# Sub-keys of two heads in the mask buffer, and four cache copies tied to expert rows, in a one-core decoder step

## What is computed

```
def peer_ffn(h, w_pq, sub_keys, expert_u, expert_v):
    t = h.shape[0]
    q = (h @ w_pq).reshape(t, PEER_HEADS, 2, PEER_D_KEY // 2)
    s = jnp.einsum('thcd,hcnd->thcn', q, sub_keys).astype(jnp.float32)
    s_top, i_top = lax.top_k(s, PEER_TOPK)
    ...
    expert = i1 * PEER_N_KEYS + i2
    g = jax.nn.softmax(c_top, axis=-1)
    u = expert_u[expert]
    act = jax.nn.gelu(jnp.einsum('thkd,td->thk', u, h))
    return jnp.einsum('thk,thkd->td', (g * act).astype(h.dtype), expert_v[expert])
```

## Time and profile before

| what | value |
|---|---|
| median of 3 runs | 1177.81 us (1176.51 to 1186.96) |
| the profiled execution's own time | 1179.88 us |
| its span | 1178.2 us |
| TensorE busy | 907.9 us (77%) |
| VectorE busy | 609.7 us (52%) |
| GpSimd busy | 409.9 us (35%) |
| moved by DMA | 481.44 MB, mean 409 GB/s |
| of it on queue q0 / q1 | 378.58 / 102.23 MB |

### The profile page before, as it was taken

How to read it: one execution, slowest core, us unless ns; L and a number is a source line. 1 busy time by engine, 2 the same in 40 slices (tenths; PEclk the granted TensorE clock), 3 DMA queues, 4 the chain that set the end, 5 groups by cost and what they waited for, 6 DMA issues and landing times.

```text
span 1178.2 us, 13121 instructions
## 1 busy us (share of the span) xinstructions
PE 907.9 (77%) x3725; PEld 425.4 (36%) x3725; DVE 609.7 (52%) x1604; ACT 333.3 (28%) x946; POOL 409.9 (35%) x432
## 2 busy tenths in 40 slices
PE   2799997678778758887877768677868777887785
PEld 0343334443334445543433434222323332333231
DVE  2200102543225625665555565566777777777766
ACT  1000004631220114323323232232333333333343
POOL 1202333122320202342434234433555445454542
PEclk9999999787988978998989898898998989989987
DMA  9999999999999998999999999999999999999997
GB/s 362 421 413 388 408 400 410 402 394 386 393 404 405 338 386 317 417 442 417 423 428 429 428 428 434 423 447 410 427 427 419 428 428 427 428 427 428 428 416 313
DMA packets 71747, 481.44 MB, mean 409 GB/s; under 512 B 9769, under 2 KB 10250, under 8 KB 26002
## 3 DMA queue, kind: packets, MB, share of 16 engines
q0 software_dynamic: 55008, 378.58, 77.8%
q1 hardware_dynamic: 16658, 102.23, 21.4%
q10 hardware_dynamic: 32, 0.02, 0.0%
HBM read 477.55 MB, written 70.32 MB: 465 GB/s over the span
## 4 chain that ended last, share of the span: by engine, by line
DMA 46%; PE 31%; issue 8%; DVE 7%; POOL 4%; ACT 3%; SPq 1%; POOLq 0%; DVEq 0%; ACTq 0%
DMA R<-in_uv,idst 33%; PE ps L1028 11%; PE ps L622 6%; DMA R<-in_sb_v,vrow 5%; POOL R L492 3%; DMA R<-in_sb_k 3%; DMA m_all<-in_subk 3%; DMA const<-in_consts 2%; DVE R L1891 2%; PE ps L912 2%; PE ps L781 2%; PE ps L649 2%; PE ps L560 1%; ACT diag L1370 1%; ACT wgt L1334 1%
## 5 line engine op out<-in xcount | busy, mean ns | idle before, releaser
L1028 PE MATMUL ps<-R,diag 128*128 128x512 f32 x1024 | 504.8, 644 | 148.3 <-ACT diag L1370 147.4
L492 POOL DMA_INDIRECT R<-in_uv,idst x256 | 300.4, 1173 | 420.1 <-PE ps L1028 357.9
L1891 DVE CUSTOM_DVE_ANT_0 R<-R,H 128x1024 f32<-128x1024 f32 x264 | 321.5, 1226 | 237.4 <-DMA R<-in_uv,idst 230.1
L1028 PEld LDWEIGHTS ps<-R,diag 128*128 128x128 f32 x1024 | 202.2, 205 | 434.4 <-issue 219.3
L1331 ACT ACTIVATE gel<-dots 128x2 f32<-128x2 f32 (+1 forms) x133 | 27.0, 203 | 414.9 <-DVE dots L1891 414.9
L622 PE MATMUL ps<-R,HT 128*128 128x512 f32 x192 | 91.8, 617 | 2.2 <-DMA R<-in_wts 2.2
L1370 ACT ACTIVATE diag<-const,wgt 128x128 f32<-128x128 f32 x256 | 89.6, 394 | 8.6
L321 POOL DMA_INDIRECT R<-in_sb_v,vrow x32 | 30.6, 958 | 99.6 <-PE ps L781 84.5
L1334 ACT ACTIVATE wgt<-gel,gst 128x1 f32<-128x1 f32 x264 | 63.4, 287 | 4.4
L312 POOL DMA_DIRECT2D R<-in_sb_k x64 | 34.8, 543 | 71.7 <-issue 71.1
L981 PE MATMUL ps<-HT,R 128*128 128x264 f32 (+1 forms) x256 | 58.2, 385 | 0.7 <-ACT HT L1089 0.7
(11 more groups left out here) (306 smaller groups left out, 802.2 us busy)
## 6 DMA issues: line engine op xcount, KB each, us to landing
R<-in_wts POOLq DMA_DIRECT2D x48, 1024.0 KB, 16.4
out_dil_k_s<-in_dil_k SPq DMA_DIRECT2D x32, 1023.5 KB
out_dil_v_s<-in_dil_v SPq DMA_DIRECT2D x32, 1023.5 KB, 7.8
R<-in_sb_k SPq DMA_DIRECT2D x64, 256.0 KB, 9.4
R<-in_sb_k POOLq DMA_DIRECT2D x64, 256.0 KB, 7.0
R<-in_win_v SPq DMA_DIRECT2D x8, 512.0 KB
R<-in_uv,idst POOLq DMA_INDIRECT x256, 12.7
R<-in_win_k SPq DMA_DIRECT2D x1, 1926.0 KB, 13.4
```

Source lines behind the costliest of these rows:

```text
L492: pool.indirect_dma_start(out=R[:, row_slot(k), :], out_offset=None, in_=A["uv"], in_offset=bass.IndirectOffsetOnAxis(ap=idst[:, par, k:k ...
L1028: last = pe.matmul(ps[:, banks + q, :], diag[:, k % 4, :], R[:, row_slot(k), D + q * 512:D + (q + 1) * 512], start=False, stop=False, skip ...
L1891: dve.tensor_tensor_reduce(u, u, H[:, t, :], 1.0, 0.0, ALU.mult, ALU.add, dots[:, k:k + 1]).then_inc(s["dot_done"], 1)
```

## The change

Two things change. First, the sub-keys of heads 1 and 2 (four of the 16 halves, 256 KB) are loaded a second time, into `msk` (then called `subk12`). POOL issues this once the eighth `oA_mm` is counted, between the gate weights 3 and 2, and the load counts up `v_ready[0]`, which the value gathers have finished with. The scores of heads 1 and 2 read `subk12`. TensorE waits for it ahead of head 1's scores, and for the full load (`subk_in`) only ahead of head 3's. The full load stays where it was, with all 16 halves. Second, `GAP` goes from 15 to 11 and `PACED` from 35 to 31: no copy stands beside the values, 20 copies run freely as before (now 11 to 30), and 33 instead of 29 are paced.

```
--- before.py
+++ after.py
@@ -60,7 +60,7 @@
 GATE1, SHIFT2, SCALE2, GATE2 = range(4)
 ROW = (0, 2, 1, 3)
 COPIES = 8 * NB
-EARLY, GAP, PACED, PACE = 11, 15, 35, 4
+EARLY, GAP, PACED, PACE = 11, 11, 31, 4
 LATE = 2
 ROWS = (4, 5, 7, 0, 1, 2, 3, 6)
 X4, NF4, NY4 = range(VECTORS, VECTORS + 3)
@@ -209,6 +209,7 @@
         WG = [R[:, s, :].rearrange("p (c n) -> p c n", c=2) for s in (4, 5, 7, 9)]
         DV = [R[:, s, 0:3 * DG].rearrange("p (g n) -> p g n", g=3) for s in (6, 7)]
         subk0 = sb("subk0", [P, 2, NKEY])
+        subk12 = msk[:, :].rearrange("p (g n) -> p g n", g=4)
         subk = m_flat[:, 0:2 * D].rearrange("p (g n) -> p g n", g=16)
         qz = Z[:, 0:2, :].rearrange("p s (c b n) -> p s c b n", c=4, b=NB)
         qz_flat = Z[:, 0:2, :].rearrange("p s (c n) -> p s c n", c=4)
@@ -268,6 +269,7 @@
         kv_ready = [sem(f"kv_ready{n}") for n in range(KVS)]
         v_ready = [sem(f"v_ready{n}") for n in range(VQ)]
         gate_ready = [kv_ready[n] for n in (1, 3, 5, 7)]
+        subk12_in = v_ready[0]
         dk_ready = [sem(f"dk_ready{n}") for n in range(len(WGROUPS))]
         dv_ready = [sem(f"dv_ready{n}") for n in range(2)]
         copied = [sem(f"copied{n}") for n in range(4)]
@@ -477,6 +479,8 @@
             query_weight(1, 8)
             pool.wait_ge(s["v_used"], NB * VQ)
             gate_weight(3, 9)
+            pool.wait_ge(s["oA_mm"], NB)
+            pool.dma_start(subk12, A["subk"][:, 2 * NKEY:6 * NKEY].rearrange("p (g n) -> p g n", g=4)).then_inc(subk12_in, 16)
             pool.wait_ge(s["vd_used"], NB)
             gate_weight(2, 7)
             pool.wait_ge(s["w_used"], QUERIES - WSLOTS)
@@ -985,11 +989,14 @@
             def score_group(h, j):
                 m = 2 * h + j
                 pe.wait_ge(s["pq_ev"], m + 1)
+                if h == 3:
+                    pe.wait_ge(s["subk_in"], 16)
                 if m >= 2:
                     pe.wait_ge(s["score_ev"], m - 1)
                 for t in range(2) if h else (1,):
                     last = pe.matmul(ps[:, 2 + j, t * P:(t + 1) * P], eq[:, j, t * P:(t + 1) * P],
-                                     subk[:, m, :] if h else subk0[:, j, :], start=True, stop=True)
+                                     (subk0 if h == 0 else subk12 if h < 3 else subk)[:, m if h > 2 else m - 2 if h else j, :],
+                                     start=True, stop=True)
                 last.then_inc(s["score_mm"], 1)
 
             def decode_scores():
@@ -1013,7 +1020,7 @@
                 for j in range(2):
                     query_group(h, j)
                 if h == 1:
-                    pe.wait_ge(s["subk_in"], 16)
+                    pe.wait_ge(subk12_in, NB * 16 + 16)
                 for j in range(2):
                     score_group(h, j)
```

## The result

| what | before | changed |
|---|---|---|
| median of 9 runs each | 1180.93 us (1176.51 to 1186.96) | 1189.62 us (1184.94 to 1193.87) |
| ratio, 95% interval | 1 | 1.0072 (1.0052 to 1.0091) |
| the profiled execution's own time | 1179.88 us | 1189.62 us |
| its span | 1178.2 us | 1187.9 us |

The change costs 0.72% of 1180.93, which is 8.5 us (6.1 to 10.7). I had forecast +2.0, and 1179.8 us in a range of 1168 to 1188. The measured 1189.62 is outside. The nine runs of the kernel before include the three that the forecast started from, and their median lies 3.1 us higher. But even without that the miss is 6.5 us, most of the 8.2 us of one term. I had also written that no change could be told, and the interval says that one can.

The account below looks back on a forecast made before the run. DMA transfers were taken to bind the kernel, with a hole in their rate at 446 to 476 us. The terms -8.2 + 0.4 + 0 + 9.8 = +2.0 us took the median from 1177.8 to 1179.8 us, range 1168 to 1188.

Parts of the forecast that it names:

- Part 1, step (b): Head 0's expert rounds: rounds 0 to 5 start early, rows are requested sooner, the 446 to 476 hole closes; -8.2 us.
- Part 1, (a): Head 0: row 7's dot and choose(1) behind it come no earlier, later by what the first paced copy takes.
- Part 2: Added 0.26 MB load on GpSimd puts gate weight 2 back 1.7 us against 1.3 slack; cost 0.4 us.
- Part 3: Four copies leave the values (206 to 244 us), where no engine waits for a transfer; worth 0.
- Part 4: Four copies join the paced ones among the experts, at the DMA ceiling, 2.46 us each; cost 9.8 us.
- A: Rival at the values: the copies did hold them up, so they end up to 9.8 us earlier; 1170.0 us, chance 0.15.
- D: Rival among the experts: the copies cost nothing there and only the hole closes; 1170.0 us, chance 0.03.
- B: Rival at head 0: TensorE binds, so the whole 17.62 us wait is saved; 1160.6 us, chance 0.05.
- C: Rival at head 0: the hole stays because VectorE sets the pace; +11.5 us, 1189.3 us, chance 0.12.

Follow-up runs that it names:

- e1: Changed kernel with the copies back where they were (GAP 15, PACED 35), leaving the sub-keys' part alone; 1182.15 us, ratio 0.9997 to the kernel before.
- e4: Changed kernel with copies back (GAP 15, PACED 35) and ScalarE's top_exp(1) moved from rank 3 to rank 7; 1175.39 us, ratio 0.9942.
- e6: Kernel before with only top_exp(1) moved from rank 3 to rank 7 in ScalarE's program of head 0; 1180.81 us, ratio 0.9986.
- e3: Changed kernel with top_exp(1) moved from rank 3 to rank 7 in ScalarE's program of head 0; 1185.28 us, ratio 1.0036.
- e7: Kernel before with the added 256 KB load, heads 1 and 2 still reading the full load behind its wait; 1181.23 us, ratio 1.0007.
- e2: Kernel before with only the copies moved (GAP 11, PACED 31); 1189.92 us, ratio 1.0070.
- e8: e4 with the added load issued behind gate weight 2 and the last two paced copies held back until e_used 258; 1177.43 us, ratio 0.9959.

## Why the prediction was wrong

**Part 1, step (b): failed.** The step read: "Rounds 0 to 5 can start as soon as their dots exist", and it ended with "So the hole closes fully" and -8.2 us. A round needs its dot, but also its gelu, weight and diagonal from ScalarE, in ScalarE's order, and in front of the diagonals of rounds 4 and 5 stands an exponential that needs `choose(1)`. I had counted `choose(1)` as a bound for VectorE and for rounds 8 and 9, and had its 12.0 us nearly right (11.8). I never asked who else waits for its result. I took the order of the waits from the trace of the kernel before, and there this wait doesn't appear, as its input was ready (457.6) when ScalarE came to it (460.37, no wait). The runs show in its place that rounds 4 and 5 start at 462.77 and that row 12 is asked for 27.9 us behind row 8 instead of 14.0, so the eight rows are asked for by 473.11 and not by 458, and the 8.2 us come out as nothing (e1: 0.9997). With the load's wait and the exponential's both removed, the term comes out near its size: e4 takes 6.9 us (4.4 to 9.2) off, where parts 1 and 2 were to take 7.8. By its interval the moved exponential alone (e6) may be worth up to 3.9 us, but its trace shows no way for it: the hole is open, and row 12 comes as long behind row 8 as without the move. One smaller size in the step was off too: the next head's rows were to be asked for near 470, and were at 474.40 in e3. The hole closed even so.

**Part 1, (a): right in the mechanism.** TensorE's first wait is gone, and `choose(1)` still starts behind the dot of row 7. It starts at 451.87 (449.45 in the earlier trace rows), which is 2.4 us later, as I had reckoned for the first paced copy. In this one trace the agreement is luck: row 7 itself was asked for 4.1 us later (424.58 against 420.50 in the earlier trace rows). Over all ten traces the time from that request to `choose(1)` is 30.3 us on average in the six without the load's wait (27.3 to 32.3) and 28.3 in the four with it (27.7 to 29.0), so row 7 does seem to come some 2 us later.

**Part 2: right within what can be measured.** +0.8 us (-1.2 to +2.8) for 0.4. The slack is small, as I had put it. Five traces have the load ahead of gate weight 2. TensorE waits for that weight in three of them (1.73 us in the changed kernel, 0.57 in e4, 0.44 in e1) and not at all in e3 and e7. The changed kernel's row, where the weight was issued at 353.97:

```profile
395.62 1.93 PE L958 MATMUL ps<-R,cT 128*32 128x256 f32 x32 [1.73 <-DMA R<-in_wts]
```

**Part 3: right.** The window 206 to 250 has a share of 0.84 where it had 1.00, and the values are no faster. GpSimd asks for the first query weight behind them at 346.1 us on average in the three traces without the copies (changed, e2, e3) and at 345.3 in the seven with them, which range from 341.8 to 349.0. TensorE's waits behind 272 in the changed kernel answer to the earlier trace rows almost to the digit:

```profile
PE ps L785 <- DMA R<-in_sb_v,vrow: 19.7, 8, 9.3
```

**Part 4: right.** Forecast 9.8 us. Measured 8.3 (5.8 to 10.9) in e2, 0.75% or 8.9 between e1 and the changed kernel, 0.94% or 11 between e4 and e3. Each of these holds part 3 too. The pace also held. SyncE's queue in the changed kernel, two copies that are eight copies apart, answers to the earlier trace rows:

```profile
702.98 0.51 SPq L361 DMA_DIRECT2D out_dil_v_s<-in_dil_v  x1
...
802.88 0.51 SPq L361 DMA_DIRECT2D out_dil_v_s<-in_dil_v  x1
```

99.9 us for 32 rows and 8 copies (98.1 before). Two pieces of the chain 16 rows apart, 929.60 and 968.92, give 78.6 us for 32 rows without copies (78.4 before).

**The rivals.** A and D are out: the copies cost their full time and gave nothing back in the values. B is out too: with the load's wait gone alone (e1) nothing was saved. C had the right picture (first round early, rate low behind it) and the right number, +11.5 for a measured +8.5, with the wrong mechanism. It blamed VectorE's pace and was to decide "once rounds 8 and 9 end after about 478". They ended by 475.81 and 477.49, when GpSimd reused their slots (475.55 and 477.24 before), and the queue had run low long before (229 GB/s from 458 to 464), for want of rows 12 to 15. Because I tied C to that one condition, I gave it 0.12 and let the range stop at 1188. The loss in this case is -0.4 (parts 1 and 2, e1) plus 8.3 (parts 3 and 4, e2), or 7.9, against 8.5 measured for both together.

## What to carry to other kernels

When a wait is taken away, walk every engine's program from that point on, in its own order, and ask of each instruction when its input is ready, above all of those that show no wait today. A late result that two engines need can hide one wait behind another, and then removing either is worth nothing and removing both is worth the whole. Moving a transfer is judged by the rate at both places: taken from a place where nobody waits for transfers it gives nothing, and put in one that runs at the ceiling it costs bytes divided by rate.

## What the runs showed that I had not expected

In the changed kernel a gate weight of 1.05 MB took from 353.97 to 395.6, some 41.6 us, beside about eleven free copies. It was also the last of six such weights and the added load, all asked for on its own queue from 345 on, and that queue moved only 7.88 MB in 345 to 391. The list of queues there:

```profile
q1 hardware_dynamic: 317, 10.81, 57.6%
q0 software_dynamic: 1129, 7.88, 44.3%
```

In e8 the expert rows fared far worse beside two copies: 16.5% of the DMA time. The packets offer a reason. There the queues moved 48 and 42 packets, nearly one for one, and those of the copies are 44 KB on average against 8 KB. The Trainium skill (DMA: Bandwidth & Descriptors, Queues, rings and completion order) says that each DMA engine goes round robin between the queues that have work, a whole packet at a time, and these counts agree with it. In 345 to 391 the counts are 317 to 1129, which does not fit it, as I noted ahead of the result. A possible reason is that q1, with at most two copies in flight, is empty for part of that stretch, but no run separates this. So a few large transfers at the wrong moment can hold up small, urgent ones by more than the average shares of a longer stretch suggest (16.5% in e8 against 44.3% here).

TensorE's second wait also cost clock. Behind the 11.86 us of idle time, rounds 4 and 5 together took 6.18 us at a mean granted clock of 0.60 (462.77 to 469.00), against 3.60 for rounds 2 and 3 at 1.00 (443.76 to 447.00). In e3 the same kind of wait (9.96 us) is followed by two rounds that take 5.50 us together at 0.67. There it costs nothing that can be seen, as the DMA engines stay full.
